# Two weight buffers and a small table at other addresses in on-chip memory

## The reference

```python
px = split_proj(hx @ w_in[l])
...
merged = sum(jax.nn.sigmoid(g) * (br @ w_branch[i])
             for i, (g, br) in enumerate(zip(gates, (r, s, f, a))))
return merged @ w_out
...
u = causal_dwconv(h @ w_up, conv_w, conv_b)
g, val = jnp.split(u, 2, axis=-1)
return (jax.nn.gelu(g) * val) @ w_down
```

## Time and profile before

| | us |
|---|---|
| runs | 1749.12, 1751.59, 1751.73; median 1751.59 |
| span of the profiled execution | 1751.7 |
| TensorE busy in it | 1709.8 (98%) |
| TensorE weight loads | 1492.3 (85%) |
| VectorE busy | 1394.4 (80%) |
| ScalarE busy | 883.4 (50%) |
| DMA | 301.32 MB, mean 172 GB/s |

### The profile page before, as it was taken

How to read it: one execution, slowest core, us unless ns; L and a number is a source line. 1 busy time by engine, 2 the same in 40 slices (tenths; PEclk the granted TensorE clock), 3 DMA queues, 4 the chain that set the end, 5 groups by cost and what they waited for, 6 DMA issues and landing times.

```text
span 1751.7 us, 28134 instructions
## 1 busy us (share of the span) xinstructions
PE 1709.8 (98%) x10612; PEld 1492.3 (85%) x10612; DVE 1394.4 (80%) x2532; ACT 883.4 (50%) x1530; POOL 0.2 (0%) x4
## 2 busy tenths in 40 slices
PE   7999999999999999999999999999999999999998
PEld 4788887777888888897888999998899888889997
DVE  7699996546789998888777699878888667778874
ACT  5322324456332233353346754567766657576563
POOL 0000000000000000000000000000000000000000
PEclk8999999999999999999999999999999999999999
DMA  9583211211766776744333388844555545346553
GB/s 339 210 293 115 87 59 48 97 37 37 248 231 241 274 255 216 240 145 144 116 102 97 95 280 311 267 136 158 187 189 181 182 153 166 113 140 208 183 189 111
DMA packets 224774, 301.32 MB, mean 172 GB/s; under 512 B 6000, under 2 KB 188656, under 8 KB 224256
## 3 DMA queue, kind: packets, MB, share of 16 engines
q1 hardware_dynamic: 224640, 299.52, 51.2%
HBM read 298.45 MB, written 1.05 MB: 171 GB/s over the span
## 4 chain that ended last, share of the span: by engine, by line
PE 48%; DVE 3%; ACT 3%; issue 2%; DMA 0%; DVEq 0%; ACTq 0%
PE bank L700 10%; PE bank L695 10%; PE bank L697 10%; PE bank L1081 3%; PE bank L1082 3%; PE bank L1083 3%; ACT w_hi L1397 1%; PE bank L671 1%; PE bank L672 1%; PE bank L673 1%; PE bank L1148 1%; PE bank L1211 1%; DVE w_lo L2178 1%; PE bank L926 0%; PE bank L1061 0%
## 5 line engine op out<-in xcount | busy, mean ns | idle before, releaser
L2178 DVE TENSOR_TENSOR w_lo<-ring,w_hi 128x1024 fp32r<-128x1024 f32 (+1 forms) x432 | 490.8, 1143 | 182.8 <-ACT w_hi L1397 179.8
L1397 ACT ACTIVATE w_hi<-ring 128x1024 fp32r<-128x1024 f32 (+1 forms) x432 | 425.5, 991 | 171.4 <-PE bank L700 92.6
L695 PE MATMUL bank<-h_hi,w_hi 128*128 128x256 f32 (+2 forms) x2086 | 378.1, 323 | 1.3 <-ACT w_hi L1397 1.0
L700 PE MATMUL bank<-h_hi,w_lo 128*128 128x256 f32 (+2 forms) x2086 | 371.1, 320 | 0.1
L697 PE MATMUL bank<-h_lo,w_hi 128*128 128x256 f32 (+2 forms) x2086 | 371.0, 320 | 0.0
L695 PEld LDWEIGHTS bank<-h_hi,w_hi 128*128 128x128 f32 x2086 | 309.0, 188 | 36.1 <-ACT w_hi L1397 2.9
L700 PEld LDWEIGHTS bank<-h_hi,w_lo 128*128 128x128 f32 x2086 | 309.8, 188 | 29.9 <-DVE w_lo L2178 0.3
L697 PEld LDWEIGHTS bank<-h_lo,w_hi 128*128 128x128 f32 x2086 | 309.8, 188 | 29.8
L1384 ACT ACTIVATE work<-bank 128x512 f32<-128x512 f32 (+1 forms) x134 | 67.3, 521 | 254.7 <-PE bank L700 173.0
L1384 ACT ACTIVATE arena<-bank 128x256 f32<-128x256 f32 (+4 forms) x119 | 55.2, 468 | 205.8 <-PE bank L700 122.9
L2479 DVE SCALAR_TENSOR_TENSOR arena<-arena,params 128x512 f32<-128x512 f32 (+1 forms) x240 | 130.7, 618 | 0.0
(11 more groups left out here) (320 smaller groups left out, 2138.6 us busy)
## 6 DMA issues: line engine op xcount, KB each, us to landing
ring<-in_w_in SPq DMA_DIRECT2D x86, 1024.0 KB, 5.5
arena<-in_ada_w_t SPq DMA_DIRECT2D x96, 512.0 KB, 6.0
ring<-in_ffn_w_up SPq DMA_DIRECT2D x44, 1024.0 KB, 5.1
ring<-in_ffn_w_down SPq DMA_DIRECT2D x20, 1024.0 KB, 5.1
ring<-in_w_branch SPq DMA_DIRECT2D x32, 512.0 KB, 4.7
arena<-in_w_mod_t SPq DMA_DIRECT2D x32, 512.0 KB, 5.2
ring<-in_gla_w_in SPq DMA_DIRECT2D x12, 1024.0 KB, 5.3
ring<-in_w_out SPq DMA_DIRECT2D x8, 1024.0 KB, 6.1
```

The source lines that it names most:

```text
L695: pe.matmul(out[:, 0:n], w[0][:, k, :], hi(k, n), start=k == 0, stop=False)
L700: m = pe.matmul(out[:, 0:n], w[1][:, k, :], hi(k, n), start=False, stop=k == tiles - 1)
L1397: nc.scalar.activation(hi, src, ACT.Copy)\
L2178: step(nc.vector.tensor_tensor(lo, src, hi.bitcast(F32), ALU.subtract), f"lo {u}", *(["used " + stream[w_units[u][0]][0]] if w_units[u][3] ...
```

## The change

The allocation of `w_hi` and `w_lo` moves behind the arena, and that of `mods` in front of them. Nothing else of the program changes: instruction by instruction, the lists of all engines are the same, with the same waits, sizes and DMAs; addresses alone differ.

```diff
-        w_parts = [sbuf(n, PARTS * KT * P, F32R)[:].rearrange("p (u t n) -> p u t n", u=PARTS, t=KT) for n in ("w_hi", "w_lo")]
-        w_hi, w_lo = ([w[:, i] for i in range(PARTS)] for w in w_parts)
-        r_hi, r_lo = ([w[:, i].rearrange("p t n -> p (t n)").rearrange("p (k n) -> p k n", k=ROW_K) for i in range(PARTS)]
-                      for w in w_parts)
...
         arena_r = sbuf("arena_r", arena_cols, F32R)
+        mods = sbuf("mods", 2 * 48 + 2 * 16 + 2 * 48 + 2 * 32 + 24 + 24)
+        w_parts = [sbuf(n, PARTS * KT * P, F32R)[:].rearrange("p (u t n) -> p u t n", u=PARTS, t=KT) for n in ("w_hi", "w_lo")]
+        w_hi, w_lo = ([w[:, i] for i in range(PARTS)] for w in w_parts)
+        r_hi, r_lo = ([w[:, i].rearrange("p t n -> p (t n)").rearrange("p (k n) -> p k n", k=ROW_K) for i in range(PARTS)]
+                      for w in w_parts)
...
         warm = sbuf("warm", 8)
-        mods = sbuf("mods", 2 * 48 + 2 * 16 + 2 * 48 + 2 * 32 + 24 + 24)
```

## The result

The changed kernel takes 1764.3 us (median of four runs, 1763.44 to 1765.12); beside it on the same chip the kernel before takes 1751.7. The ratio is 1.0076, with a 95% interval of 1.0063 to 1.0088: slower by 12.6 us, where 1765 was forecast. The sum came out; two of its terms did not, as the rows show.

The account below looks back on a forecast made before the run. The prediction took TensorE, busy 98% of the span, as the bound, its time set by the step between matmuls. +14.9 - 1.3 = +13.6 us on 1751.7 gave 1765, range 1725 to 1768.

Parts of the forecast that it names:

- The cause: TensorE's matmul pace: differs with the moving operand's address less that of weights loading beside it, modulo 256; 226.7 or 231.7 ns.
- Step (1a): 512-column matmuls at offset 0, 2,980 taken as settled: go from 226.7 to 231.7 ns, +15 us.
- the prediction's own sign: Layer 0 and merge stretches of 512 columns: eight matmuls take 1.85 us in place of 1.81 if the forecast is right.
- Step (1b): 256-column matmuls from the arena at offset 0: go from 120 to 117.5 ns, -1.3 us; at 113, -3.5.
- Steps (2) and (3): Moves of work, stats, c2_row, small and warm by 64, and of mods: cost 0 in other engines, 1 us either way.
- Settles one step lower: Settled 512-column matmuls drop to 220 ns, -23 us, with 256 columns -3.5: 1725 us; chance 0.20.
- one step higher: 512-column matmuls run at 233.3 ns throughout, +21 us: 1773 us with 256 columns unchanged; chance 0.14.
- no change: 512 columns stay at 226.7 ns, 256 columns give 0 to -3.5 us: 1750 us; chance 0.16.

Follow-up runs that it names:

- the first three experiments: Against the kernel before: weights behind the arena without the 64 bytes, 1751.3 us; all buffers later together, 1751.5 us; only work, stats, c2_row, small, warm and mods moved, 1751.7 us.
- the run with the other buffers alone: Against the kernel before, mods behind the arena so that work, stats, c2_row, small, warm and mods move while h, weights and arena stay: 1751.7 us, ratio 1.0003.
- the kernel with x at 192: Kernel before with the second block's tokens x_hi and x_lo one after the other, 192 bytes into their buffer: 1740.5 us, ratio 0.9938.

## Why the prediction was right, and where it was not

**What bounds the kernel** was read rightly: what a matmul lost, the span lost, and the other engines' times did not change.

**The cause** was read rightly. Rows 3 against rows 4 left open whether the layer, the step of k or the offset makes the difference; the first three experiments close that, and the one with half the weights shows the price moving with the offset inside one tile. The Trainium skill ("SBUF — State Buffer", section "Who interferes with whom") gives TensorE's two reads independent ports, and by that the change should have done nothing. This case does not agree: 226.7 against 233.3 ns for one instruction, by the distance of the two addresses alone.

**Step (1a), the price of 512 columns, was mis-sized.** The prediction took 231.7 ns, unsettled, for 192 and 64 alike, since stepping stretches run at it and in rows 5 each offset lasts three matmuls "without coming under it". That reading was too coarse: from start to start the matmuls of rows 5 take 226 to 236 ns, and 231.7 is only the mean. A stepping stretch has a price of its own, changes of offset among it: 231.8 holds neither for 192 (233.3) nor for 64 (228.9). The sequences do settle, at 192 on the value given as the upper bound, which was a rival with a chance of 0.14. "No row stays there" was a weak reason against it, as no row had the offset at all. Nor did the prediction's own sign come, 1.85 us for eight: it is 1.87. In place of +15 us the term is 16.2 + 1.2 = +17.4.

**Step (1b) was mis-sized** the other way: 113.7 ns and not 117.5, so -3.5 us, the lower bound given, and not -1.3. That bound came from rows 9, whose two values at one offset, 113 and 117.5, are the two paces that the later runs show; the prediction took the one that the stepping stretches have too.

The two errors, +2.5 and -2.2, nearly cancel, which is why 1765 met 1764.3: the mechanism and the sign were read rightly, but that the sum fits to a microsecond is luck. The range from 1725 to 1768 held gains as well as losses, so that the time alone would have told little; the steps from start to start do. **Steps (2) and (3)** at nothing were right, by the run with the other buffers alone.

**The rivals.** "Settles one step lower" holds for 256 columns and fails for 512; "one step higher" holds for 512 columns in column products and not for row products; "no change" falls by the result's interval. The forecast had the two widths going opposite ways, but at the unsettled pace; neither it nor a rival had them settle, 512 columns higher and 256 lower, which is what happened.

## What to carry to other kernels

Where matmuls follow each other without a pause and each loads weights of its own, let every tile of the moving operand and of the weights start at a fixed distance modulo 256, and choose it by width: here 0 for 512 columns, 192 for 256 (which brought most sequences to 113.3 ns, and not all). Tiles padded by 64 bytes, so that the distance steps, gave away 4 ns in 117 and 5 in 232. Read the pace from starts in the timeline, in stretches of two dozen matmuls, and make sure that a sequence has settled before its value is multiplied.

## What was not expected

**Two steady paces at one offset.** With 256 columns at 64 or 192, a sequence keeps 113.3 or 117.8 ns to its end: two sequences of over a thousand matmuls kept 113.3 at 192, and two kept 117.8 at 64. Which of the two it is seems decided in the first dozen.

**Steps of 6.67 ns.** The settled means 113.3, 120, 226.7 and 233.3 are 17, 18, 34 and 35 times 6.67 ns, and that is the time of 16 columns, 64 bytes, at 2.4 GHz if a column takes a cycle, as 425 ns for 512 columns at 1.2 GHz, below, would have it. Other means don't lie there: 228.9 is that of 226, 229 and 232 in turn, 117.8 that of distances of 117 to 119, and 232.5 and 118.3 are none of them either. Even the 233.3 of the change is about 231 and 236 in turn. Why the paces are these is open.

**Nothing on top at the lower clock.** At the start of layer 1 TensorE waits 1.95 us, and soon after that the profile before has half the clock granted. Timeline, and busy times with the granted clock (the third column from the right):

```profile
800.18 0.63 PE L673 MATMUL bank<-h_hi,w_lo 128*128 128x512 f32 x1
...
801.88 0.63 PE L671 MATMUL bank<-h_hi,w_hi 128*128 128x512 f32 x1
```

```profile
800.00:802.00 2.00, 2.00 (x6) 1.52 (x6) 2.00 (x5) 0.00 (x0) 0.00 (x0) 0.50 0.00 0
```

Four steps in 1.70 us are 425 ns, about 512 columns at 1.2 GHz (426.7) and nothing more, in a stretch with stepping offsets. So what costs some 18 ns a matmul at the full clock in the earlier trace rows costs nothing here. The Trainium skill ("TensorE: Matmul & The Clock Gate", section "Wait — 56ns, not 53.3ns?") has the same for the lower clock, and 2.5 ns on top at the higher one; here 13.3 to 20 are on top of 512 columns, in matmuls that each load weights in the rounded format.

**The clock does not always fall there.** In the kernel with x at 192 the same wait, 1.96 us, is followed by the full clock:

```profile
796.00:798.00 2.00, 1.78 (x8) 1.48 (x9) 2.00 (x6) 0.38 (x1) 0.00 (x0) 1.00 0.50 176
```

By the starts of the same instructions in the two traces that saves some 1.5 us. The clock stayed up there in six of this study's thirteen profiles, this one among them, and fell in seven; differences of one or two microseconds between single profiles say nothing here.
